# One addition over eight heads for the candidate sums of the expert selection

## The chip, the cores and the metric

The kernel runs on one core of a Trainium2 chip. Its time is the device time of one launch in microseconds (us), as the median of several runs. A core has a matrix engine (PE), a vector engine (DVE), an activation engine (ACT), a general engine (POOL, GpSimd) and a queue engine (SP) that here only issues transfers. Each works through its own list of instructions in order, and they wait for one another by semaphores.

## The reference, cut to what matters

Two layers of a decoder trunk over 256 tokens of width 1024. Each layer ends with a feed-forward part of 128 x 128 = 16384 experts of one neuron each, of which every head of every token picks 16:

```
q = (ht @ wq).reshape(T, 8, 2, 64)
s1, s2 = q[:, :, 0] @ keys1.T, q[:, :, 1] @ keys2.T      # (T, 8 heads, 128 keys) each
v1, i1 = top_k(s1, 16);  v2, i2 = top_k(s2, 16)
cand = (v1[..., :, None] + v2[..., None, :]).reshape(T, 8, 256)
cv, ci = top_k(cand, 16)
a, b = take(i1, ci // 16), take(i2, ci % 16);  e = a * 128 + b
g = softmax(cv)
out = sum over heads and picks of g * gelu(u_tab[e] . ht) * v_tab[e]
```

The change concerns the line `cand`: for each token and head, all 16 x 16 sums of a value of the first list and one of the second.

## The kernel before, in words

The kernel does not gather experts. It computes gelu(u . h) for all 16384 experts and all 256 tokens, weighs this table with the softmax weights of the picked ones (zero elsewhere), and multiplies by the whole of v. So the weights of u and v stream through the core once a layer, as "pieces" of 128 x 512 numbers. SP loads pairs of pieces into four buffers `raw`. ACT rounds a piece to its high part (`hi_piece`, L500, into one of four slots `w_hi`), POOL subtracts to get the low part (L454, into one of four slots `w_lo`), and PE multiplies both parts. A slot is written again only when PE has counted the piece in it as used.

A key is one row of 128 experts: two pieces. In the u phase PE runs 24 products a key (L1066 to L1068; 12 a piece) into one of four accumulators, and ACT reads the key's result out through gelu (`key_out`, L655) into the table `experts`. ACT's list for the u phase is, key by key: read out key k, round one piece, round the next. PE may use an accumulator again when the key four before has been read out.

While PE, ACT and POOL go through the first 64 keys of u, DVE does the selection, for token tile 0 (tokens 0 to 127, on the 128 partitions) and then for token tile 1. For each tile: 16 rounds of maxima over 128 keys (L1536 to L1540), a copy of the indices as numbers (L1541), the eight candidate sums (L1543 to L1545, one a head), eight rounds of maxima over the 256 candidates (L1550 to L1554), four small operations on the indices (L1556 to L1559), and for each of the two lists a comparison with 0 to 15, a product and a sum over 128 x 16 x 16 elements (L1561, L1564, L1565), which look up the picked key. Then DVE takes the maxima of the picked values and subtracts them (L1568, L1569); that sets the semaphore `cv_ready`.

The exponential of the softmax is ACT's. It stands in ACT's list at a fixed place: after key 51 has been read out and the next two pieces are rounded (`EXP_AT = 52`), ACT waits for `cv_ready` (L676), computes the exponential (L677), calls gelu on a dummy value so that gelu's table is there again (L660), and goes on with key 52. DVE sums and divides (L1571 to L1573) and sets `w_ready`. PE waits for that after key 55 (`SLOTS_AT = 56`), transposes the picked indices and weights (L767, six products), and goes on with keys 56 to 63. DVE makes the first one-hot tables (L1593, L1601, L1607) out of the transposes, which PE uses from key 64 on (L1034), between the keys of the second half of u, and likewise in the first half of v.

Every DVE operation of the selection is issued with `d.step`, which waits for the operation before the next is issued.

Of the kernel before, what the change touches and what calls it, by code (L numbers as in the profile page):

```python
# [25 lines left out]
ALU = mybir.AluOpType  # L26
# [4 lines left out]
P = 128  # L31
# [10 lines left out]
PH, KEYS, TOPK = 8, 128, 16  # L42
# [119 lines left out]
def trunk(nc, x, mem, stream, cols, parb, parr, lnrow, zgw, consts, pm, tril, out):  # L162
    ctx = ExitStack()
    with ctx:
# [101 lines left out]
        cand = rout[:, :].rearrange("p (h i j) -> p h i j", h=PH, i=TOPK)  # L266
# [7 lines left out]
        tv = topv[:, :].rearrange("p (h f k) -> p h f k", h=PH, f=2)  # L274
# [51 lines left out]
        PRIMED = dict(layer_free=2, u_out=4, g_out=2, acc_free0=1, acc_free1=1)  # L326
        sig = {n: Signal(sem(n), per, PRIMED.get(n, 0)) for n, per in PER.items()}
        n_uses = [sum(b == k for _, b in USES) for k in range(4)]
        filled = [Signal(sem(f"aux{b}_filled"), n_uses[b]) for b in range(4)]
        drained = [Signal(sem(f"aux{b}_drained"), n_uses[b], 1) for b in range(4)]  # L330
# [13 lines left out]
        def bank(name):  # L344
            return aux[:, turn[name][0], :]
# [759 lines left out]
        def _(dve):  # L1105
            V = nc.vector
# [45 lines left out]
            with dve.Fori(0, DEPTH) as layer:  # L1152
                d = Engine(dve, layer, dve_step)
# [371 lines left out]
                for t in range(T):  # L1525
                    for i in range(4):
                        use = f"ps{t}_{i}"
                        d.wait_filled(use)
                        d.step(V.tensor_copy(rs[:, 2 * i:2 * i + 2], bank(use).rearrange("p (h f k) -> p h f k", h=2, f=2)),
                               drains=use)  # L1530

                    for h in range(PH):
                        for f in range(2):
                            v = rs[:, h, f, :]
                            d.settle()
                            d.step(V.max(tv[:, h, f, 0:8], v))  # L1536
                            d.step(V.max_index(ti[:, h, f, 0:8], tv[:, h, f, 0:8], v))
                            d.step(V.match_replace(v, tv[:, h, f, 0:8], v, LOWEST))
                            d.step(V.max(tv[:, h, f, 8:16], v))
                            d.step(V.max_index(ti[:, h, f, 8:16], tv[:, h, f, 8:16], v))  # L1540
                    d.step(V.tensor_copy(topf[:], topi[:]))  # L1541

                    for h in range(PH):  # L1543
                        d.step(V.tensor_tensor(cand[:, h], tv[:, h, 0, :].unsqueeze(2).broadcast_to((P, 16, 16)),
                                               tv[:, h, 1, :].unsqueeze(1).broadcast_to((P, 16, 16)), ALU.add))  # L1545
                    for h in range(PH):
                        v = cand[:, h].rearrange("p i j -> p (i j)")
                        c = ci[:, h * 16:(h + 1) * 16]
                        w = cv[:, t, h, :]
                        d.step(V.max(w[:, 0:8], v))  # L1550
                        d.step(V.max_index(c[:, 0:8], w[:, 0:8], v))
                        d.step(V.match_replace(v, w[:, 0:8], v, LOWEST))
                        d.step(V.max(w[:, 8:16], v))
                        d.step(V.max_index(c[:, 8:16], w[:, 8:16], v))  # L1554

                    d.step(V.tensor_scalar(cia, ci, 4, None, ALU.logical_shift_right))  # L1556
                    d.step(V.tensor_copy(iab[:, 0, :], cia))
                    d.step(V.tensor_scalar(cia, ci, 15, None, ALU.bitwise_and))
                    d.step(V.tensor_copy(iab[:, 1, :], cia))  # L1559
                    for f in range(2):  # L1560
                        d.step(V.tensor_tensor(onehot, iab[:, f, :].unsqueeze(2).broadcast_to((P, 128, 16)),  # L1561
                                               iota16.unsqueeze(1).broadcast_to((P, 128, 16)), ALU.is_equal))
                        oh = onehot.rearrange("p (h k) j -> p h k j", h=PH)
                        d.step(V.tensor_tensor(oh, oh, tf[:, :, f, :].unsqueeze(2).broadcast_to((P, PH, 16, 16)), ALU.mult))  # L1564
                        d.step(V.tensor_reduce(ab[:, f, t].rearrange("p h k -> p (h k)"), onehot, AX.X, ALU.add))  # L1565
# [229 lines left out]
```

How the kernel before makes its waits and increments, by code:

```python
            def wait(self, name, k=None):  # L357
                s = sig[name]
                self.e.wait_ge(s.sem, self.value(s, s.per if k is None else k))
# [1 line left out]
            def wait_filled(self, use):  # L362
                b, j = turn[use]
                self.e.wait_ge(filled[b].sem, self.value(filled[b], j + 1))
# [1 line left out]
            def wait_drained(self, use):  # L367
                b, j = turn[use]
                self.e.wait_ge(drained[b].sem, self.value(drained[b], j + 1))
# [1 line left out]
            def wait_bank_free(self, use):  # L372
                b, j = turn[use]
                self.e.wait_ge(drained[b].sem, self.value(drained[b], j))
# [1 line left out]
            def wait_block(self, block):  # L377
                i = BLOCKS.index(block)
                s = sig[f"acc_free{i % 2}"]
                self.e.wait_ge(s.sem, self.value(s, i // 2 + 1))
# [1 line left out]
            def wait_pieces(self, n):  # L383
                self.e.wait_ge(used, self.layer * PIECES + (SLOTS + n))
# [5 lines left out]
            def step(self, ins, name=None, drains=None, block=None):  # L391
# [10 lines left out]
                    s.sent += 1  # L402
                    self.wait_block(block)
                elif name is not None:
                    s = sig[name]
                    ins.then_inc(s.sem, 1)
                    s.sent += 1
                    self.e.wait_ge(s.sem, self.value(s, s.sent))
                else:
                    self.n += 1
                    ins.then_inc(self.own, 1)
                    self.e.wait_ge(self.own, self.n)
```

## Time and profile before

| what | us |
|---|---|
| median of 3 runs | 2434.26 |
| lowest and highest | 2433.69, 2434.85 |
| the profiled execution, its own time | 2432.56 |
| its span, first to last instruction | 2430.8 |

The profile is of that one execution. Busy shares of the span are: PE 94%, POOL 72%, DVE 58%, ACT 48%. The rows further down come from its trace. A row of a timeline is the start of an instruction in us from the span's start, its duration, engine, line and operation, and, in brackets, how long its engine sat idle before it and who released it. Matmuls are pipelined: a duration of 0.28 us with starts 0.12 us apart means one product every 0.12 us. The two layers are one loop in the program, so each line appears twice in time: layer 0 does its u phase from about 385 us, layer 1 from about 1588 us.

### The profile page before, as it was taken

How to read it: one execution, taken by the hardware profiler on the slowest of the kernel's cores; microseconds unless marked ns; L12 is line 12 of the kernel's file. 1: busy time of each engine (PE TensorE's matmuls, PEld its weight loads, DVE VectorE, ACT ScalarE, POOL GpSimd, SP SyncE). 2: the span in 40 equal slices, each digit the busy share in tenths (PEclk: the TensorE clock that was granted, in tenths of full speed). 3: DMA queues.
4: the chain of work that ended last, by engine and by line, in shares of the span. 5: the costliest groups of instructions: out<-in, count | busy, mean ns of one | idle time of the engine just before them, and what ended most of it. 6: DMA issues, size and time to landing. Idle time of an engine off the chain costs nothing.

```text
span 2430.8 us, 51319 instructions
## 1 busy us (share of the span) xinstructions
PE 2295.4 (94%) x15530; PEld 2032.3 (84%) x15530; DVE 1419.0 (58%) x2318; ACT 1167.6 (48%) x2273; POOL 1747.7 (72%) x1316
## 2 busy tenths in 40 slices
PE   6999879998999999999989997899899999999998
PEld 5887768998999888888868776699899998888887
DVE  4545347995656677733345453489945556776333
ACT  5445544454444444456543554544444444444564
POOL 4745746997777777788866566579877777777886
PEclk9999989999999999999998998999999999999999
DMA  6423424554444444455554334345444444444654
GB/s 228 155 89 113 141 93 130 165 180 136 150 142 151 139 155 148 154 199 190 189 203 135 105 115 137 97 142 168 155 147 149 144 149 145 155 148 155 203 188 153
DMA packets 100517, 367.12 MB, mean 151 GB/s; under 512 B 11472, under 2 KB 11984, under 8 KB 100176
## 3 DMA queue, kind: packets, MB, share of 16 engines
q1 hardware_dynamic: 97040, 353.41, 44.3%
q10 hardware_dynamic: 3392, 12.66, 1.4%
q8 instruction: 42, 0.69, 0.1%
q14 instruction: 43, 0.35, 0.0%
HBM read 364.98 MB, written 1.05 MB: 151 GB/s over the span
## 4 chain that ended last, share of the span: by engine, by line
PE 44%; issue 2%; DVE 2%; POOL 1%; ACT 1%; POOLq 0%; DVEq 0%; ACTq 0%
PE acc L1066 5%; PE acc L1068 5%; PE acc L1067 5%; PE acc L1095 5%; PE acc L1097 5%; PE acc L1096 5%; PE aux L1034 4%; PE acc L805 3%; PE acc L807 3%; PE acc L806 3%; PE aux L767 1%; POOL w_lo L454 1%; PE aux L917 0%; PE aux L852 0%; DVE h_lo L1157 0%
## 5 line engine op out<-in xcount | busy, mean ns | idle before, releaser
L454 POOL TENSOR_TENSOR w_lo<-raw,w_hi 128x512 fp32r<-128x512 f32 x1312 | 1747.5, 1343 | 670.8 <-ACT w_hi L500 575.8
L500 ACT ACTIVATE w_hi<-raw 128x512 fp32r<-128x512 f32 x1344 | 840.8, 628 | 913.5 <-PE acc L1068 468.9
L1066 PE MATMUL acc<-h_hi,w_hi 128*128 128x256 f32 x2048 | 588.9, 288 | 30.8 <-POOL w_lo L454 30.8
L1068 PE MATMUL acc<-h_hi,w_lo 128*128 128x256 f32 x2048 | 580.5, 283 | 0.0
L1067 PE MATMUL acc<-h_lo,w_hi 128*128 128x256 f32 x2048 | 580.5, 283 | 0.0
L1066 PEld LDWEIGHTS acc<-h_hi,w_hi 128*128 128x128 f32 x2048 | 395.7, 193 | 33.7 <-POOL w_lo L454 33.3
L1095 PE MATMUL acc<-w_hi,eg 128*128 128x512 f32 x1024 | 406.2, 397 | 1.2 <-DVE eg L1623 1.2
L1097 PE MATMUL acc<-w_hi,eg 128*128 128x512 f32 x1024 | 399.6, 390 | 0.0
L1096 PE MATMUL acc<-w_lo,eg 128*128 128x512 f32 x1024 | 398.7, 389 | 0.0
L1067 PEld LDWEIGHTS acc<-h_lo,w_hi 128*128 128x128 f32 x2048 | 394.7, 193 | 0.1
L1068 PEld LDWEIGHTS acc<-h_hi,w_lo 128*128 128x128 f32 x2048 | 394.0, 192 | 0.0
L1593 DVE TENSOR_TENSOR hot_b<-aux,sel 128x1024 bf16<-128x1024 f32 x128 | 156.8, 1225 | 292.0 <-PE aux L1034 291.9
L1623 DVE TENSOR_TENSOR eg<-big,eg 128x256 fp32r<-128x256 f32 x256 | 177.8, 694 | 234.7 <-ACT eg L684 233.6
L805 PE MATMUL acc<-w_hi,h_hi 128*128 128x512 f32 x576 | 247.2, 429 | 34.0 <-POOL w_lo L454 25.3
L807 PE MATMUL acc<-w_hi,h_lo 128*128 128x512 f32 x640 | 255.8, 400 | 0.0
L806 PE MATMUL acc<-w_lo,h_hi 128*128 128x512 f32 x576 | 229.1, 398 | 0.0
L1095 PEld LDWEIGHTS acc<-w_hi,eg 128*128 128x128 f32 x1024 | 194.1, 190 | 39.8 <-POOL w_lo L454 2.1
L1097 PEld LDWEIGHTS acc<-w_hi,eg 128*128 128x128 f32 x1024 | 192.2, 188 | 41.6
L1096 PEld LDWEIGHTS acc<-w_lo,eg 128*128 128x128 f32 x1024 | 192.6, 188 | 38.3
L684 ACT ACTIVATE eg<-big 128x256 fp32r (+1 forms) x256 | 106.7, 418 | 207.4 <-PE acc L1097 207.4
L805 PEld LDWEIGHTS acc<-w_hi,h_hi 128*128 128x128 f32 x576 | 111.3, 193 | 65.5 <-issue 31.2
L807 PEld LDWEIGHTS acc<-w_hi,h_lo 128*128 128x128 f32 x640 | 123.8, 193 | 27.8
(229 smaller groups left out, 2411.9 us busy)
## 6 DMA issues: line engine op xcount, KB each, us to landing
raw<-stream_dram SPq DMA_DIRECT2D x672, 512.0 KB, 3.3
big<-parb_dram ACTq DMA_DIRECT2D x2, 2128.0 KB, 9.6
big<-mem_dram ACTq DMA_DIRECT2D x3, 1024.0 KB, 5.3
big<-pm_dram ACTq DMA_DIRECT2D x2, 768.0 KB, 14.0
big<-parr_dram ACTq DMA_DIRECT2D x2, 640.0 KB, 10.8
X<-x_dram ACTq DMA_DIRECT2D x1, 1024.0 KB, 12.0
out_dram<-X SPq DMA_DIRECT2D x1, 1024.0 KB, 4.0
big<-lnrow_dram ACTq DMA_DIRECT2D x2, 256.0 KB, 11.5
```

Source lines behind the costliest of these rows:

```text
L454: nc.gpsimd.tensor_tensor(w_lo[:, k % SLOTS, :], raw[:, k // PER_CHUNK, k % PER_CHUNK, :], w_hi[:, k % SLOTS, :].bitcast(F32), ALU.subtrac ...
L500: nc.scalar.activation(w_hi[:, k % SLOTS, :], raw[:, (k // PER_CHUNK) % RAW, k % PER_CHUNK, :], ACT.Copy).then_inc(hi_ready, 1)
L805: pe_.matmul(dst, r_hi[:, kt, ts], w_hi[:, slot, :], start=(k == 0), stop=False)
L806: pe_.matmul(dst, r_hi[:, kt, ts], w_lo[:, slot, :], start=False, stop=False)
L807: ins = pe_.matmul(dst, r_lo[:, kt, ts], w_hi[:, slot, :], start=False, stop=(k == depth - 1))
L1066: pe_.matmul(acc[:, q, 0:S], wh, h_hi[:, kt, :], start=(kt == 0), stop=False)
L1067: pe_.matmul(acc[:, q, 0:S], wh, h_lo[:, kt, :], start=False, stop=False)
L1068: ins = pe_.matmul(acc[:, q, 0:S], w_lo[:, r % SLOTS, k * P:(k + 1) * P], h_hi[:, kt, :], start=False, stop=(kt == KD - 1))
L1095: pe_.matmul(dst, eg[:, q % 2, 0, ts], w_hi[:, slot, :], start=False, stop=False)
L1096: pe_.matmul(dst, eg[:, q % 2, 0, ts], w_lo[:, slot, :], start=False, stop=False)
L1097: ins = pe_.matmul(dst, eg[:, q % 2, 1, ts], w_hi[:, slot, :], start=False, stop=False)
L1623: V.tensor_tensor(eg[:, q % 2, 1, :], src, eg[:, q % 2, 0, :].bitcast(F32), ALU.subtract).then_inc(sig["eg_ready"].sem, 1)
```

## The change

The eight additions of one head (256 sums on each partition) for a token tile become one addition over all eight heads (2048 sums on each partition). Both inputs are read through the same kind of broadcast pattern as before, with the head as one more dimension; what is written, and where, is the same.

```
-                    for h in range(PH):
-                        d.step(V.tensor_tensor(cand[:, h], tv[:, h, 0, :].unsqueeze(2).broadcast_to((P, 16, 16)),
-                                               tv[:, h, 1, :].unsqueeze(1).broadcast_to((P, 16, 16)), ALU.add))
+                    d.step(V.tensor_tensor(cand, tv[:, :, 0, :].unsqueeze(3).broadcast_to((P, PH, TOPK, TOPK)),
+                                           tv[:, :, 1, :].unsqueeze(2).broadcast_to((P, PH, TOPK, TOPK)), ALU.add))
```

Over the whole kernel that is 32 additions (8 heads, 2 tiles, 2 layers) before and 4 after.

## Rows read from the trace of the kernel before

**Rows 1.** The page's busy times: us (share of the span) and instructions.
```profile
PE 2295.4 (94%) x15530; PEld 2032.3 (84%) x15530; DVE 1419.0 (58%) x2318; ACT 1167.6 (48%) x2273; POOL 1747.7 (72%) x1316
```

**Rows 2.** The view of waits: who waited for whom, total us, times, longest us.
```profile
PE acc L1066 <- POOL w_lo L454: 30.8, 12, 8.3
...
ACT sel L677 <- DVE sel L1569: 21.5, 2, 10.8
```

**Rows 3.** ACT's timeline around the exponential, layer 0.
```profile
543.52 0.37 ACT L655 ACTIVATE big<-acc 128x256 f32<-128x256 f32 x1
...
544.42 0.63 ACT L500 ACTIVATE w_hi<-raw 128x512 fp32r<-128x512 f32 x1 [0.53 <-PE acc L1068]
...
546.66 1.28 ACT L677 ACT_TABLE_LOAD   x1
558.70 0.42 ACT L677 ACTIVATE sel<-sel 128x256 f32<-128x256 f32 x1 [10.76 <-DVE sel L1569]
...
561.00 0.38 ACT L655 ACTIVATE big<-acc 128x256 f32 x1 [0.36 <-ACT cst L660]
561.28 1.14 ACT L500 ACTIVATE w_hi<-raw 128x512 fp32r<-128x512 f32 x2
```

**Rows 4.** ACT's timeline, more readouts of keys, layer 0 and then layer 1.
```profile
454.72 0.37 ACT L655 ACTIVATE big<-acc 128x256 f32 x1
...
474.40 0.37 ACT L655 ACTIVATE big<-acc 128x256 f32 x1
...
578.12 0.37 ACT L655 ACTIVATE big<-acc 128x256 f32 x1
...
1745.95 0.37 ACT L655 ACTIVATE big<-acc 128x256 f32<-128x256 f32 x1
...
1780.12 0.37 ACT L655 ACTIVATE big<-acc 128x256 f32 x1
```

**Rows 5.** PE's timeline, layer 0: the first product behind a gap.
```profile
456.93 0.39 PE L1066 MATMUL acc<-h_hi,w_hi 128*128 128x256 f32 x1
...
460.20 0.39 PE L1066 MATMUL acc<-h_hi,w_hi 128*128 128x256 f32 x1 [1.58 <-POOL w_lo L454]
...
563.30 0.58 PE L1066 MATMUL acc<-h_hi,w_hi 128*128 128x256 f32 x1 [8.27 <-POOL w_lo L454]
```

**Rows 6.** DVE's timeline in the selection, layer 0, tile 0; last row tile 1.
```profile
417.49 11.62 DVE L1544 TENSOR_TENSOR big<-sel 128x256 f32<-128x256 f32 x8
429.14 0.43 DVE L1550 MAX8 sel<-big 128x8 f32<-128x256 f32 x1
...
449.24 1.27 DVE L1556 TENSOR_SCALAR big<-big 128x128 uint32<-128x128 uint32 x1
...
453.42 2.29 DVE L1561 TENSOR_TENSOR big<-sel,cst 128x2048 f32<-128x2048 f32 x1
455.75 3.27 DVE L1564 TENSOR_TENSOR big<-big,sel 128x2048 f32<-128x2048 f32 x1
...
461.38 3.42 DVE L1561 TENSOR_TENSOR big<-sel,cst 128x2048 f32<-128x2048 f32 x1
...
558.24 0.42 DVE L1569 TENSOR_TENSOR sel<-sel,st 128x256 f32<-128x256 f32 x1
```

**Rows 7.** Windows: length, busy PE, PEld, DVE, ACT, POOL (instructions), granted clock, DMA.
```profile
417.00:429.20 12.20, 12.20 (x104) 12.20 (x103) 11.89 (x10) 6.79 (x14) 10.90 (x10) 1.00 0.59 180
453.40:470.50 17.10, 12.74 (x101) 12.02 (x100) 16.87 (x7) 6.14 (x12) 17.05 (x8) 1.00 0.29 95
558.00:575.00 17.00, 11.70 (x83) 11.70 (x84) 7.66 (x13) 8.90 (x18) 11.17 (x9) 0.72 0.29 94
```

**Rows 8.** The chain that ended last, layer 1: start us, us, what.
```profile
1659.26 3.33 POOL w_lo L454
...
1764.40 1.28 POOL w_lo L454
...
1770.27 0.65 PE aux L767 x6
```

## The prediction

> **What bounds the kernel now.** The page's busy times come first: PE is busy 94% of the span and no other engine over 72% [rows 1], so a change on DVE pays only where PE waits, at the end of a chain, for DVE. The view of waits shows that place. ACT waits 21.5 us in two pieces (one a layer) for DVE's L1569 before the exponential, and PE waits 30.8 us for POOL's low parts in the u phase, the longest single wait 8.3 us [rows 2]. ACT's timeline ties the two: in layer 0 ACT has loaded the exponential's table by 546.66 + 1.28 = 547.94 and then sits idle 10.76 us until 558.70 [rows 3]. Behind it in its list stand the rounding of the next pieces and the readout of key 52; with no high parts POOL has nothing to subtract, and PE stands still 8.27 us until 563.30 [rows 5]. So the selection is on the path here: it reaches L1569 too late for ACT.
>
> What the late exponential costs is read from the readouts of keys. Undisturbed, a key takes 24 products x 0.12 = 2.88 us, 1.44 us a piece. From the readout of key 51 to that of key 58 are seven keys, 20.16 us; in layer 0 it took 578.12 - 543.52 = 34.60, in layer 1 1780.12 - 1745.95 = 34.17 [rows 3, 4]. Less 0.65 us for the transposes that belong there [rows 8], PE lost 13.79 and 13.36 us, together **27.15 us**. This holds the look-up's own stalls in tile 1, the wait, and the slow products after the wait: in 558 to 575 us the granted clock is 0.72, a mix of 2.4 and 1.2 GHz, after PE had stood still 8.27 us [rows 5, 7].
>
> One more loss has to be known, since it will move. In the look-up of tile 0 (four operations over 2048 elements with two inputs in the same memory), PE is busy 12.74 of 17.10 us while POOL is busy throughout [rows 7]. A low part takes 1.28 us undisturbed and 3.33 beside such an operation [rows 8]: DVE's operation holds POOL up 2.05 us. In keys: from 454.72 to 474.40 are five keys, 14.40 us, and it took 19.68 [rows 4], so PE lost **5.28 us**.
>
> **The change part by part.** *Removed:* eight additions a tile. They take 417.49 to 429.14, 11.65 us, 1.46 each [rows 6]. Their own work is small: L1569, the same 256 sums while ACT's wait leaves POOL idle, takes 0.42 [rows 6]. The other 1.0 us each is waiting: every addition waits for POOL's current low part to end. POOL is hardly held up, and PE is busy 12.20 of 12.20 us in that stretch [rows 7]; so the eight cost only DVE's time.
>
> *Added:* one addition over 2048 elements. The trace has the shape in L1561 and L1564, L1564 with the same four-dimensional pattern: 2.29 where DVE came first, 3.27 and 3.42 where it had to wait for POOL's current low part [rows 6]. The additions start when POOL has just begun a low part (they take 1.46 each for that reason), so I take 3.42; the ends are 2.29 and 3.42. DVE saves 11.65 - 3.45 = 8.2 us a tile (9.3 at the other end), 16.4 a layer.
>
> *What DVE's 16.4 us do.* L1569 ends at 558.66 - 16.4 = 542.3, while ACT is not ready for it before 547.94 [rows 3, 6]. ACT's wait of 10.76 goes altogether, with 5.6 us to spare; 16.4 us don't pay as 16.4.
>
> *What is late next.* First, the look-up of tile 1 now lies before key 51 instead of largely under ACT's wait: it costs what tile 0's costs, 5.28 us a layer (which moves ACT's turn later by as much and adds to the margin). Second, the exponential itself stays in ACT's list: table load at 546.66, 1.28; exponential 0.42; from its start to the next readout 561.00 - 558.70 = 2.30 [rows 3]. Without the wait the readout of key 52 comes at 547.94 + 2.30 = 550.24 and the next rounding 0.28 later, 550.52. Undisturbed, key 52's readout would come 2.88 us behind key 51's, at 546.40, and the rounding another 544.42 - 543.52 = 0.90 later, at 547.30 [rows 3]: it is 3.2 us late. Of that a cushion takes some: from the start of a rounding to PE's use of the piece is 563.30 - 561.28 = 2.02 us [rows 3, 5], and with four slots PE has three other pieces to do, 4.32 us, so 2.2 to 2.3 us of delay go unseen. PE loses 1.0 us (bounds 0 and 3.2).
>
> Third, the new addition holds POOL up once for 2.05 us, against that same cushion of 2.2. The row for this is the first L1561 of tile 0, which meets a full cushion: PE starts at 456.93 without a wait worth a bracket, and only the second long operation gives the gap of 1.58 [rows 5, 6]. I take 0.2 us a tile; bounds 0 and 2.05. Before the look-up follows, the rounds of maxima last 20.1 us (429.14 to 449.24 [rows 6]), 14 pieces in which POOL regains 1.44 - 1.28 = 0.16 each, 2.2 together: the cushion is full again. Fourth, L1569, L1571 and L1573 now run beside a busy POOL: 0.2 us a layer, 0 to 1.
>
> The Trainium skill bears on the third point: "SBUF — State Buffer", section "SBUF: two separate sides", has the port pair that DVE and GpSimd share as an exclusive lock, held for the whole instruction, with the loser fully blocked. The trace agrees in both directions (1.46 against 0.42 for DVE, 3.33 against 1.28 for POOL), and the rule speaks against this change, for one long hold replaces eight short ones that fitted between POOL's instructions. What it would do without the cushion is rival B.
>
> *Sum.* A layer now loses 5.28 + 1.0 + 2 x 0.2 + 0.2 = 6.88 where it lost 13.79 and 13.36; gain 27.15 - 13.76 = **13.4 us**. The profiled execution took 2432.56 (span 2430.8 and 1.76 around it), so 2419.2; it lies 1.70 below the median of the runs, which I carry over: 2434.26 - 13.4 = **2420.9 us**. Terms at their good ends: the 5.28 stay, all else 0: gain 16.6, 2417.7. The v phase, the projections and the second half of u are not touched: PE sets their pace, and they only start earlier.
>
> **The rivals.**
>
> *B, the long hold is paid in full.* The new addition costs PE all of 2.05 us a tile, because the cushion is not full where it stands. For: the second long operation of each look-up pays 1.58 [rows 5]. Against: PE runs without a gap before and during the eight additions [rows 7], so the cushion should be full. Gain 13.4 - 4 x 1.85 = 6.0: 2428.3.
>
> *C, the gain is eaten.* B, and the look-up of tile 1 also finds no cushion, because POOL does not regain it in the rounds of maxima: 2.2 us more in each of four look-ups, 6.0 - 8.8 = -2.8, or a part of it: about 2435, no change. For: POOL's margin is only 0.16 us a piece. Against: tile 0's look-up pays 5.28 for four holds of 2.05, so it begins with a cushion.
>
> *D, slower: the 1.46 us is the addition's own time for this pattern and not waiting.* Then one instruction holds POOL 8 x 1.40 = 11.2 us; PE loses 11.2 - 2.2 = 9.0 a tile, 36.0 in all. DVE comes no earlier, but PE and ACT come so much later that ACT's wait is gone too: 27.15 - 2 x 6.28 = 14.6 back. Net 21.4 slower: 2455.7. It decides from a hold of 2.2 + 14.6 / 4 = 5.9 us. For: the same line takes 1.40 all along. Against: L1569's 0.42 and L1564's 3.27 for eight times the elements.
>
> *E, more:* the cushion also hides the exponential, and the moved look-up falls partly into it: gain 17 to 20, 2416.
>
> **How the numbers follow.** What a measurement of this kernel tells from no change is about 0.2%, 4.9 us. Forecast (gain 9 to 17) 0.70; B (gain 3 to 9) 0.14, of which 0.10 is over 4.9; C 0.06; D 0.04; E 0.06. Faster 0.70 + 0.10 + 0.06 = 0.86, no change 0.04 + 0.06 = 0.10, slower 0.04. The range is the forecast's with B's value and the good end: 2416.5 to 2428.5.
>
> **What would show it.** Right: L1544 once a tile at 2.3 to 3.5 us; no idle of ACT before L677 for DVE; no PE gap over 2 us in keys 52 to 55, and no granted clock below 1.00 there; three gaps of 1.2 to 1.6 at tile 1's look-up as at tile 0's; a gap of about 1 us behind the exponential. Wrong: a gap of PE behind the new addition (B), or the addition at 6 us or more (D); the prediction fails as well if the time that PE gains in the first half of u comes back as waits later.

## The result, and the profile after

The changed kernel takes 2419.74 us (median of 4 runs, 2415.87 to 2421.91) against 2434.18 us before (2433.69 to 2434.85): a ratio of 0.9939 with a 95% interval of [0.9922, 0.9956], 14.4 us less. Predicted were 2420.9 us, in a range of 2416.5 to 2428.5. The profiled execution took 2418.69 us, 13.87 less than that of before.

The page's busy times of the changed kernel, beside [rows 1]: PE keeps its work, DVE does 30 us less.

```profile
PE 2290.8 (95%) x15526; PEld 2028.1 (84%) x15530; DVE 1389.0 (57%) x2290; ACT 1167.2 (48%) x2273; POOL 1756.9 (73%) x1316
```

The view of waits, beside [rows 2]. ACT's wait for DVE before the exponential is no longer in it. It stands the other way round: DVE now waits for ACT's exponential, 13.0 us in each layer, and nobody waits for DVE there.

```profile
DVE st L1570 <- ACT sel L677: 26.0, 2, 13.0
...
PE acc L1066 <- POOL w_lo L454: 19.8, 14, 1.6
```

ACT's timeline, layer 0, beside [rows 3]. The exponential follows its table without a bracket, that is without idle time; the readout of key 52 comes 6.58 us behind key 51's, where it came 17.48 behind it before.

```profile
547.09 0.37 ACT L655 ACTIVATE big<-acc 128x256 f32<-128x256 f32 x1
...
550.08 1.28 ACT L677 ACT_TABLE_LOAD   x1
551.38 0.42 ACT L677 ACTIVATE sel<-sel 128x256 f32<-128x256 f32 x1
...
553.67 0.38 ACT L655 ACTIVATE big<-acc 128x256 f32 x1 [0.37 <-ACT cst L660]
...
568.98 0.37 ACT L655 ACTIVATE big<-acc 128x256 f32 x1
```

DVE's timeline, layer 0, beside [rows 6]: the one addition in tile 0, the first maximum behind it, the comparison and the product of tile 1's first look-up, and L1568, which is L1569 of before.

```profile
415.46 3.40 DVE L1543 TENSOR_TENSOR big<-sel 128x2048 f32<-128x2048 f32 x1
418.90 0.43 DVE L1549 MAX8 sel<-big 128x8 f32<-128x256 f32 x1
...
521.48 2.29 DVE L1560 TENSOR_TENSOR big<-sel,cst 128x2048 f32<-128x2048 f32 x1
523.81 3.27 DVE L1563 TENSOR_TENSOR big<-big,sel 128x2048 f32<-128x2048 f32 x1
...
537.80 1.10 DVE L1568 TENSOR_TENSOR sel<-sel,st 128x256 f32<-128x256 f32 x1
```

PE's timeline, layer 0, beside [rows 5]: three gaps in tile 1's look-up and a short one behind the exponential. The gap of 8.27 us is gone.

```profile
528.25 0.39 PE L1066 MATMUL acc<-h_hi,w_hi 128*128 128x256 f32 x1 [1.58 <-POOL w_lo L454]
...
532.90 0.39 PE L1066 MATMUL acc<-h_hi,w_hi 128*128 128x256 f32 x1 [1.52 <-POOL w_lo L454]
...
536.17 0.39 PE L1066 MATMUL acc<-h_hi,w_hi 128*128 128x256 f32 x1 [1.58 <-POOL w_lo L454]
...
555.98 0.39 PE L1066 MATMUL acc<-h_hi,w_hi 128*128 128x256 f32 x1 [0.83 <-POOL w_lo L454]
```

The windows, beside [rows 7]: the new addition (PE without a gap), the look-ups of tile 0 and tile 1, and the stretch of the exponential, where the granted clock is now 1.00 and not 0.72.

```profile
415.00:419.00 4.00, 4.00 (x36) 4.00 (x35) 3.93 (x3) 2.16 (x5) 3.71 (x3) 1.00 0.65 204
442.00:460.00 18.00, 13.63 (x109) 12.92 (x107) 17.76 (x8) 6.77 (x13) 17.81 (x9) 1.00 0.31 105
522.00:540.00 18.00, 13.32 (x106) 12.60 (x105) 16.67 (x8) 6.77 (x13) 17.97 (x8) 1.00 0.33 107
549.00:560.00 11.00, 10.17 (x86) 9.97 (x85) 1.44 (x4) 8.30 (x15) 7.75 (x7) 1.00 0.45 151
```

What PE lost in the u phase, by the readouts of keys as in the prediction (time between two readouts, less 2.88 us a key, less 0.65 for the transposes), in us; layer 1 in brackets where it differs by over 0.1:

| kernel | look-up tile 0 | look-up tile 1 | wait and exponential | sum of a layer |
|---|---|---|---|---|
| before | 5.28 | in the next column | 13.79 (13.36) | 19.07 (18.66) |
| after | 5.28 | 5.59 | 1.08 | 11.95 |

The difference of the two layers' sums is 7.12 + 6.71 = 13.8 us.

### The profile page after: what moved, and what is told of

It is laid out like the page before. It is cut to its first block, busy times and chain, and to the rows that moved or that the text cites. A ratio compares the mean times of both kernels' runs of the same rounds, so it can differ in the third digit from the quotient of the medians.

```text
span 2416.9 us, 51287 instructions
## 1 busy us (share of the span) xinstructions
PE 2290.8 (95%) x15526; PEld 2028.1 (84%) x15530; DVE 1389.0 (57%) x2290; ACT 1167.2 (48%) x2273; POOL 1756.9 (73%) x1316
## 4 chain that ended last, share of the span: by engine, by line
PE 44%; issue 2%; DVE 2%; POOL 1%; ACT 1%; POOLq 0%; DVEq 0%; ACTq 0%
PE acc L1066 5%; PE acc L1095 5%; PE acc L1068 5%; PE acc L1067 5%; PE acc L1097 5%; PE acc L1096 5%; PE aux L1034 4%; PE acc L805 3%; PE acc L807 3%; PE acc L806 3%; POOL w_lo L454 1%; PE aux L767 1%; PE aux L852 0%; PE aux L1020 0%; PE aux L917 0%
```

## The experiments

Two theories were set against each other. *ACT's turn*: the gain comes from DVE being ready before ACT reaches the exponential, and from nothing else. *Contention*: it comes from DVE holding up POOL less often. The times of one kernel lie some us apart from run to run (the last section has a likely part of the reason), so the losses in keys are given beside the medians. The kernel before was timed again with each group: 2431.75 us beside the first four kernels (2427.45 to 2436.64), 2434.54 beside the last three.

**Half the change.** One addition in tile 0, eight in tile 1.

```
+                    if t == 0:
                         d.step(V.tensor_tensor(cand, ...))       # all heads
+                    else:
+                        for h in range(PH):
+                            d.step(V.tensor_tensor(cand[:, h], ...))
```

> One addition in token tile 0 only, the eight additions stay in tile 1. Theory ACT's turn: the gain is that DVE's selection is done before ACT comes to the exponential; after the full change the margin was 12.46 us (L1568 ends at 538.90, ACT's table is loaded at 551.36), so giving back 8.2 us of it costs nothing: time as after the full change, 2419.7 (2416 to 2423), no idle of ACT before the exponential. Rival contention: the gain is that fewer DVE operations hold up POOL; then half the change gives half the gain, about 2427.

Measured: 2418.0 us, ratio 0.9953 [0.9939, 0.9968]. ACT does not wait, PE loses 11.66 us a layer (11.95 after the full change). ACT's timeline in layer 0 of this kernel:

```profile
546.15 1.28 ACT L677 ACT_TABLE_LOAD   x1
547.45 0.42 ACT L677 ACTIVATE sel<-sel 128x256 f32<-128x256 f32 x1
```

Half of the change has the whole of the gain: the second 8.2 us that DVE saves buy nothing. (The 0.3 us between 11.66 and 11.95 are tile 1's look-up, which costs 5.29 here and 5.59 after the full change; its second comparison waits for POOL here, 3.43 us, and comes before POOL's low part there, 2.29.) This speaks against contention, which expected 2427.

**The exponential later, additions as before.**

```
-EXP_AT, SLOTS_AT = 52, 56
+EXP_AT, SLOTS_AT = 56, 60
```

> The kernel before with all its eight additions a tile, and only the exponential's place in ACT's list moved from behind key 51 to behind key 55, PE's transposes from behind key 55 to behind key 59. Theory ACT's turn: ACT comes four keys (11.5 us) later and has the look-up's stalls in front of it, so its wait of 10.76 us goes and most of the gain comes without any change to the additions: 2420 to 2424 (up to 1.5 us a layer may be lost at key 64, since DVE has four keys less for the one-hot tables). Rival contention: 2434, as before.

Measured: 2417.92 us, ratio 0.9947 [0.9928, 0.9967], 13.8 us less than the kernel before beside it; 2420 to 2424 had been expected from a kernel before of 2434. No idle before the exponential, 12.27 us lost a layer: 5.29 and 6.36 in the look-ups and behind the exponential, and 0.62 at key 64, where PE waits 0.5 us for DVE's one-hot table (a wait of 0.5 us a layer on L1607 is in this kernel's view of waits and neither in that of the kernel before nor in that of the changed one). So two numbers in the program, with no change of the additions, give nearly the same as the change. Contention expected 2434 here.

**DVE's time given back with operations that do not hold up POOL.** The first maximum of each head (L1549) repeated, 18 more a tile.

```
+                        for _ in range((4, 3, 3, 4, 3, 3, 3, 3)[h]):
                             d.step(V.max(w[:, 0:8], v))
```

> The changed kernel with 18 maxima (0.43 us each and 0.03 between) repeated in each tile, 8.3 us a tile: as long for DVE as the saving, but these do not hold up POOL. Theory ACT's turn: ACT waits again, about 10 us a layer, and the time is that of the kernel before, 2434 (2431 to 2437). Rival contention: as the changed kernel, 2420.

Measured: 2431.42 us, ratio 0.9999 [0.9985, 1.0013]. ACT waits as before:

```profile
560.87 0.42 ACT L677 ACTIVATE sel<-sel 128x256 f32<-128x256 f32 x1 [10.75 <-DVE sel L1569]
```

PE loses 19.1 us in layer 0, as in the kernel before (19.07). The one addition is in place here, and the gain is gone with DVE's time alone. With the two kernels above, this settles the question for *ACT's turn*.

**The long hold, doubled.** The prediction charged the new addition's hold of POOL at 0.2 us a tile, because a cushion takes it.

```
+                    for _ in range(2):
                         d.step(V.tensor_tensor(cand, ...))
```

> The changed kernel with its one addition done twice in a row in each tile (the second writes the same sums). DVE is 3.4 us later a tile, within the margin. Theory ACT's turn with a cushion of 2.2 us between POOL and PE: the first hold of 2.05 us stays unseen as in the changed kernel, the second is paid at 1.6 to 2.05 us, four times: 6 to 8 us slower than the changed kernel, 2426 to 2428, and PE shows one gap of about 1.6 us behind each pair. Rival, no cushion at work (a hold of POOL is never paid by itself): 2420.

Measured: 2423.69 us, ratio 0.9965 [0.9954, 0.9976]; 5.7 us more than the half change and the later exponential, which were timed beside it. That is a little less than the 6 to 8 expected. DVE's pair and the gap of PE that follows it, layer 0, tile 0:

```profile
414.30 6.71 DVE L1544 TENSOR_TENSOR big<-sel 128x2048 f32<-128x2048 f32 x2
```

```profile
422.19 0.38 PE L1066 MATMUL acc<-h_hi,w_hi 128*128 128x256 f32 x1 [1.48 <-POOL w_lo L454]
```

In keys, 419.86 to 424.47 are 4.61 us for one key: 1.73 lost in each tile, where the changed kernel, with one hold, loses nothing (418.14, 421.02, 423.90: 2.88 each). The first hold is hidden, the second is paid nearly in full. The look-ups behind it cost 5.28 and 5.29, no more than without it, so POOL regains the cushion during the maxima, as the prediction had it. A layer loses 15.1 us in all, 3.2 more than after the change: twice 1.73, less the 0.3 that tile 1's look-up costs less here.

**The look-ups without the hold.** If POOL's hold is the whole of the look-ups' loss, it must go when the long operations have one input in PSUM, the memory that PE's results are written to (here `acc` and `aux`), and only one in SBUF, where the other tiles lie. That needs PSUM banks that PE leaves alone, so the key scores of tile 1 are copied out early. A control has that alone.

```
                 for t in range(T):
                     for i in range(4):
-                        d.step(V.tensor_copy(rs[:, 2 * i:2 * i + 2], ...), drains=use)
+                        d.step(V.tensor_copy((rs, rs2)[t][:, 2 * i:2 * i + 2], ...), drains=use)
+                for t in range(T):
                     (selection of tile t, from (rs, rs2)[t])
```

> Control for the next two: the changed kernel, with the key scores of tile 1 copied out of PSUM right behind those of tile 0 into a buffer of their own, so that PSUM's upper banks are free during both tiles' selections. Nothing else. DVE has the same work in another order, with 12.46 us of margin: as the changed kernel, 2416 to 2422, the same three gaps of PE in each look-up (5.3 and 5.6 us).

Measured: 2415.49 us, ratio 0.9923 [0.9906, 0.994], just under the expected range; 11.96 us lost a layer, as after the change. Then the look-up's inputs:

```
-        tf = topf[:, :].rearrange(...)
-        iab = topv[:, :].rearrange(...)
+        tf = aux[:, 3, 0:256].rearrange(...)
+        iab = aux[:, 2, 0:256].rearrange(...)
...
-                    d.step(V.tensor_copy(topf[:], topi[:]))
+                    d.step(V.tensor_copy(aux[:, 3, 0:256], topi[:]))
```

> e5_early_scores, and the copies of the indices (L1541) and of the candidate positions (L1556, L1558) write to PSUM instead of SBUF, so that each 2048-element operation of the look-ups has one input in PSUM and one in SBUF. Theory (two SBUF inputs of a long DVE operation hold up POOL, and that is the whole of PE's loss in the look-ups): the gaps of PE in both look-ups go, 5.28 + 5.59 us a layer, 21.7 us in all; DVE's operations take 2.2 to 2.5 us without waiting; the one addition still holds POOL once, unseen; the exponential's 1.08 stays. Time 2395 to 2400. Rival (the look-ups' loss comes from DVE's long operations as such, or from ACT or the transfers): the gaps stay, 2416 to 2422.

Measured: **2398.32 us**, ratio 0.9854 [0.9837, 0.987] to the kernel before. DVE's first comparison and product of tile 0 (L1562 and L1565 here) take 2.29 us each, without waiting:

```profile
447.04 2.29 DVE L1562 TENSOR_TENSOR big<-aux,cst 128x2048 f32<-128x2048 f32 x1
449.37 2.29 DVE L1565 TENSOR_TENSOR big<-big,aux 128x2048 f32<-128x2048 f32 x1
```

and the windows of both look-ups show PE without a gap, where it was busy 12.74 of 17.10 us in [rows 7]:

```profile
444.00:461.00 17.00, 17.00 (x144) 17.00 (x143) 16.60 (x11) 8.93 (x19) 15.43 (x12) 1.00 0.53 181
515.00:532.00 17.00, 17.00 (x144) 17.00 (x143) 16.62 (x12) 9.21 (x18) 15.27 (x13) 1.00 0.51 185
```

1.16 us are lost in layer 0, of which 1.08 behind the exponential. DVE does operations over the same 2048 elements, so it is not long operations as such, nor ACT or the transfers: it is two inputs in SBUF. (The same kernel has three copies ahead of these operations write to PSUM; what that alone is worth was not measured.) By the keys this gives back 10.8 us a layer against the control, 21.6 in all; the profiled executions of the two differ by 19.35 us and the medians by 17.2. Of what is missing in the profiled executions, 1.5 us are there before the u phase of layer 0, which begins that much later in this one (first readout at 391.85 and not 390.32); the rest is not explained. This kernel is faster than the kernel before and the changed one.

**The same with the eight additions back.**

> e6_lookup_psum with the eight additions of one head back in both tiles. DVE is 8.2 us later a tile, but no longer waits for POOL in the look-ups (about 1.0 us in three of four operations, 3 a tile), and PE comes earlier. ACT's turn: DVE is ready about 6 us earlier than before the change, ACT as early as then, so a wait of 4 to 5 us stays and PE loses 5 to 8 us a layer where e6 loses 1.08: 8 to 14 us slower than e6. Rival contention: as e6.

Measured: 2415.47 us, ratio 0.9928 [0.9911, 0.9945]; 17.2 us slower than the kernel above, more than the 8 to 14 expected. The wait is 6.73 us, and PE stands still behind it:

```profile
537.98 1.28 ACT L678 ACT_TABLE_LOAD   x1
545.99 0.42 ACT L678 ACTIVATE sel<-sel 128x256 f32<-128x256 f32 x1 [6.73 <-DVE sel L1571]
```

```profile
550.59 0.58 PE L1067 MATMUL acc<-h_hi,w_hi 128*128 128x256 f32 x1 [7.54 <-POOL w_lo L455]
```

In keys it loses 10.37 us in layer 0 and 9.27 in layer 1. What the expectation missed: counted from the start of the u phase (387.57 us before, 384.32 here), ACT's table is there 5.4 us earlier, for tile 0's look-up no longer holds PE up, and DVE is ready 9.5 us earlier, not 6. Of the wait of 10.76 us, 10.76 + 5.4 - 9.5 = 6.7 stay. Of DVE's 9.5 us the comparisons and products give 6.1 (12.22 us a tile before, 4 x 2.29 here) and the four small operations ahead of them 2.4: two of these are copies that now write to PSUM, and the second takes 0.29 us where it took 1.35 (L1559). The same change of the additions is worth 13.8 us by the keys in the one surrounding and 17.3 in the other.

## Why the prediction was right

*The additions' time was waiting for POOL.* The same 256 sums that took 0.42 us with POOL idle [rows 6] take 1.10 in the changed kernel (L1568), where POOL is busy at that moment. The eight additions met POOL in that way; for the first of them in the kernel before, the rows are:

```profile
417.45 1.30 POOL L454 TENSOR_TENSOR w_lo<-raw,w_hi 128x512 fp32r<-128x512 f32 x1
...
417.49 1.54 DVE L1544 TENSOR_TENSOR big<-sel 128x256 f32<-128x256 f32 x1
```

POOL's low part ends at 418.75, the addition that began 0.04 us after it at 419.03.

*The one addition takes 3.42 us.* Measured: 3.27 to 3.40 over the four; in layer 0, tile 0, the first maximum behind it starts 8.21 us earlier against the additions' start than before.

*16.4 us for DVE don't pay as 16.4.* DVE is ready at 538.90, ACT's table at 551.36: a margin of 12.46 us, predicted as 5.6 and the look-up's 5.28 on top, 10.9. Half the change shows that the surplus is worth nothing, the repeated maxima that the missing 8.3 us a tile are worth everything.

*What is late next.* Tile 1's look-up costs 5.59 us a layer (predicted 5.28, by a row in which the second comparison waits for POOL; here it comes first), the exponential 1.08 (1.0), the long hold 0.00 (0.2 a tile), the small operations nothing that could be seen (0.2 a layer). Sum: 13.8 us gained against 13.4; part of the closeness is that the look-up came out dearer and the two small terms cheaper. Rival B's price was near (1.73 us for a hold that is not hidden, 2.05 forecast), but its condition does not hold: the cushion is full where the addition stands. Rival C falls with it, D with the addition's 3.4 us, and E because the exponential's 1.08 us stay and the moved look-up costs no less than tile 0's.

The Trainium skill's rule of the exclusive lock ("SBUF — State Buffer", section "SBUF: two separate sides") is borne out in its details too: it counts a DVE operation with two SBUF inputs, and with one input moved to PSUM the hold is gone, for DVE (2.29 us instead of 3.27 and 3.42) and for POOL and PE.

*By luck?* The median's gain, 14.4 us, is nearer to 13.4 than the runs deserve: they spread over 6 us. The agreement that counts is that of the losses in keys: the look-up of tile 0 (5.28 to 5.30) and the exponential (1.08) come out the same in every kernel that has them undisturbed.

## What to carry to other kernels

When an engine waits for another at a fixed place of its list, look for the margin, not for the saving: beyond the wait's length a shorter chain is worth nothing, and moving the place may do the same without touching the chain (here two constants). Many short DVE operations with two SBUF inputs each wait for GpSimd's instruction of the moment, 1.0 us for 0.42 us of work; one long one waits once, but holds GpSimd up by nearly its own length (2.05 us by an operation of 2.29), so ask how much delay the queue behind GpSimd can take, and whether a second such operation follows. Moving one input of the long operations to PSUM removed both sides of it.

## What the runs showed of the hardware that was not expected

The key scores are 32 products of PE ahead of the u phase (L1020). In layer 0 they take 9.48 us before and 7.17 after; in layer 1 it is the other way round, 7.17 and 9.51. The change has no part in it: the granted clock differs, in this window 0.57 before and 1.00 after. The first row is of the kernel before, the second of the changed one.

```profile
378.00:384.00 6.00, 5.55 (x15) 4.56 (x16) 2.06 (x4) 0.00 (x0) 0.00 (x0) 0.57 0.00 1
```

```profile
378.00:384.00 6.00, 5.28 (x24) 4.67 (x25) 4.01 (x8) 0.00 (x0) 0.00 (x0) 1.00 0.00 1
```

0.57 is mostly the lower of the two levels, 1.2 GHz, and it comes in a stretch where PE has just been idle on and off for DVE and ACT (busy 15.20 of the 18 us ahead before, 14.93 after, with granted clocks of 0.95 and 1.00); as that is much the same in both, why it falls in one and not in the other stays open. Each time it falls there costs about 2.3 us. In these two executions it fell once each, so the two cancel: the u phase of layer 0 begins 2.02 us earlier after the change, and that of layer 1 gives 1.8 of it back. The traces of the other seven kernels agree: the 32 products take 7.17 or 7.18 us in the one layer and 9.48 to 9.53 in the other, in six of them; in the seventh, the repeated maxima (2437.69 us, the slowest execution profiled), they take 9.5 in both. So a stretch that meets the drop in one execution and not in another is a likely part of why single runs of one kernel lie some us apart (2427.45 to 2436.64 for the kernel before). It is not the whole: the 32 products of layer 0 begin anywhere between 375.08 and 380.54 us in the nine traces, though no change of the program lies ahead of them, and what makes that is not shown. It is the reason to read a gain of this size in the stage, by the distances of the keys, and not from two medians alone.
